# Attention with the values stationary in the array's column halves, outputs transposed, probabilities divided before use, and one more pipeline step

## The reference

```python
def swa_sink_attention(x, w_qkv, b_qkv, sinks, w_out):     # 32 query heads of 64, 4 key/value heads
    h = x @ w_qkv + b_qkv
    ...
    scores = jnp.einsum('bnikgd,bnjkd->bnkgij', q, kb).astype(jnp.float32) * ATTN_HEAD_DIM ** -0.5
    ...                                                      # blocks of 128 tokens, window 128
    scores = jnp.where(valid[None, :, None, None], scores + bias[None, None], -jnp.inf)
    m = jnp.maximum(jnp.max(scores, axis=-1, keepdims=True), sink)
    p = jnp.exp(scores - m)
    probs = p / (jnp.sum(p, axis=-1, keepdims=True) + jnp.exp(sink - m))
    o = jnp.einsum('bnkgij,bnjkd->bnikgd', probs.astype(vb.dtype), vb)
    return o.reshape(B, S, ATTN_Q_WIDTH) @ w_out
```

## Time and profile before

| | |
|---|---|
| Median of three runs | 2091.2 us |
| The profiled execution | 2091.75 us, its span 2090.0 us |
| PE busy | 2066.4 us, 99% of the span |
| DVE, ACT busy | 1416.5 us (68%), 887.2 us (42%) |
| Granted TensorE clock, mean | 0.997 of full |
| Attention stage (first S to the last turned output) | 1141.4 to 1290.2 us |

### The profile page before, as it was taken

How to read it: one execution, slowest core, us unless ns; L and a number is a source line. 1 busy time by engine, 2 the same in 40 slices (tenths; PEclk the granted TensorE clock), 3 DMA queues, 4 the chain that set the end, 5 groups by cost and what they waited for, 6 DMA issues and landing times.

```text
span 2090.0 us, 27045 instructions
## 1 busy us (share of the span) xinstructions
PE 2066.4 (99%) x10886; PEld 1761.2 (84%) x10886; DVE 1416.5 (68%) x1589; ACT 887.2 (42%) x813; POOL 5.8 (0%) x10
## 2 busy tenths in 40 slices
PE   8999999999999999999999999999999999999997
PEld 7888888888888888888878888888888888888886
DVE  5445366867767677676786665786776777766768
ACT  4443434543434344344434554454343434434342
POOL 0000000000000000000000000000000000000000
PEclk9999999999999999999999999999999999999999
DMA  8664464755555655555545434566555555555552
GB/s 310 211 193 151 140 242 146 249 193 197 183 197 182 196 185 192 189 187 195 184 165 187 134 108 168 175 213 216 195 183 198 182 197 184 193 188 188 193 184 98
DMA packets 193915, 390.30 MB, mean 187 GB/s; under 512 B 6377, under 2 KB 8643, under 8 KB 192835
## 3 DMA queue, kind: packets, MB, share of 16 engines
q1 hardware_dynamic: 193571, 389.24, 55.8%
q10 hardware_dynamic: 288, 0.26, 0.0%
HBM read 387.12 MB, written 2.10 MB: 186 GB/s over the span
## 4 chain that ended last, share of the span: by engine, by line
PE 97%; DVE 2%; ACT 1%; DMA 0%; issue 0%; DVEq 0%; ACTq 0%
PE ps L1137 17%; PE ps L1140 17%; PE ps L1138 17%; PE ps L1150 13%; PE ps L1152 13%; PE ps L1151 13%; PE ps L1126 1%; PE ps L1493 1%; PE ps L1200 0%; PE ps L1476 0%; PE ps L1162 0%; PE ps L1127 0%; PE ps L1337 0%; PE ps L1469 0%; PE ps L1467 0%; PE ps L1466 0%
## 5 line engine op out<-in xcount | busy, mean ns | idle before, releaser
L441 ACT ACTIVATE w_hi<-raw 128x2048 fp32r<-128x2048 f32 x355 | 679.8, 1917 | 956.7 <-DMA raw<-ffn_w_in 519.9
L699 DVE TENSOR_TENSOR w_lo<-raw,w_hi 128x2048 fp32r<-128x2048 f32 x355 | 808.2, 2287 | 249.2 <-ACT w_hi L441 248.6
L1138 PEld LDWEIGHTS ps<-T,w_lo 128*128 128x128 f32 x3136 | 589.2, 188 | 138.3
L1137 PE MATMUL ps<-T,w_hi 128*128 128x512 f32 x1568 | 621.0, 396 | 0.0
L1140 PE MATMUL ps<-T,w_hi 128*128 128x512 f32 x1568 | 620.2, 396 | 0.0
L1138 PE MATMUL ps<-T,w_lo 128*128 128x256 f32 x3136 | 616.1, 278 | 0.0
L1137 PEld LDWEIGHTS ps<-T,w_hi 128*128 128x128 f32 x1568 | 297.7, 190 | 4.5 <-issue 3.7
L1140 PEld LDWEIGHTS ps<-T,w_hi 128*128 128x128 f32 x1568 | 293.8, 187 | 0.0
L1150 PE MATMUL ps<-w_hi,gT 128*128 128x512 f32 x672 | 261.5, 389 | 0.0
L1152 PE MATMUL ps<-w_hi,gT 128*128 128x512 f32 x672 | 261.4, 389 | 0.0
L1151 PE MATMUL ps<-w_lo,gT 128*128 128x512 f32 x672 | 261.4, 389 | 0.0
(11 more groups left out here) (135 smaller groups left out, 971.1 us busy)
## 6 DMA issues: line engine op xcount, KB each, us to landing
raw<-ffn_w_in SPq DMA_DIRECT2D x176, 1024.0 KB, 5.0
raw<-ffn_w_out SPq DMA_DIRECT2D x88, 1024.0 KB, 5.0
raw<-even_w_in SPq DMA_DIRECT2D x39, 1024.0 KB, 5.1
raw<-attn_w_qkv SPq DMA_DIRECT2D x20, 1024.0 KB, 5.2
raw<-even_w_out SPq DMA_DIRECT2D x16, 1024.0 KB, 5.1
raw<-attn_w_out SPq DMA_DIRECT2D x16, 1024.0 KB, 5.0
arena<-ln_gain SPq DMA_DIRECT2D x4, 1024.0 KB, 7.0
arena<-ln_bias SPq DMA_DIRECT2D x4, 1024.0 KB, 9.0
```

The source lines that it names most:

```text
L441: nc.scalar.activation(w_hi[:, s % RING], raw[:, s % RING], ACT.Copy).then_inc(hi_ready, 1)
L699: vec.tensor_tensor(w_lo[:, s % RING], raw[:, s % RING], w_hi[:, s % RING].bitcast(F32), ALU.subtract).then_inc(lo_ready, 1)
L1137: mm(ps[:, bank], w_hi[:, s % RING, k, c], T[:, t], start=first, stop=False)
L1138: ins = mm(ps[:, bank, 0:SEQ], w_lo[:, s % RING, k, c], T[:, t, 0:SEQ], start=False, stop=False)
```

## The change

V swaps its operands: the values are stationary (64 columns, so half of the array's columns) and `PT` moves (128 columns). The two heads of a pair take the two column halves: their outputs go to partitions 0 to 63 and 64 to 127 of a bank, one bank for each block of queries. The result is thus already transposed, and one DVE copy takes it to `oT`; the 32 turns of the output on PE are gone. Since the sum's reciprocal now would belong to columns, DVE divides the exponentials by their sums before T (new semaphore `att_normed`), and V comes a burst later (pair b-3, T pair b-2), with `S` in two buffers. The output projection's first four tiles go to `gT`, its order and banks change, the splits of the output read `oT`, and the copy of the last query tiles' first half starts from a semaphore of its own.

```diff
-ODD_OUT_ORDER = [(0, 0), (0, 1), (1, 0), (1, 1), (0, 2), (1, 2), (2, 0), (0, 3), (1, 3), (2, 1), (2, 2), (2, 3)] + \
+ODD_OUT_ORDER = [(0, 0), (1, 0), (0, 1), (1, 1), (0, 2), (1, 2), (2, 0), (2, 1), (0, 3), (1, 3), (2, 2), (2, 3)] + \
...
-ODD_OUT_BANKS = [0, 2, 6, 0]
-ODD_OUT_ENDS = {8: 0, 9: 1, 12: 2}
+ODD_OUT_BANKS = [0, 2, 4, 0]
+ODD_OUT_ENDS = {9: 0, 10: 1, 12: 2}
...
-ATT_FILL_AT = {0: 0, 1: 2, 4: 4, 6: 6}
+ATT_FILL_AT = {-7: [0], -5: [1], 0: [2, 3], 1: [4], 3: [5], 5: [6], 7: [7]}
...
-BURSTS = PAIRS + 2
+BURSTS = PAIRS + 3
...
+        att_tiles = lambda j: (gT if j < 2 else T)[:, 2 * j:2 * j + 2]
...
-                act.wait_ge(used, ended + turn * 12)
+                if n == TP_ODD + 7:
+                    act.wait_ge(queries_half, 1)
+                else:
+                    act.wait_ge(used, ended + turn * 12)
...
-                if 0 <= b - 1 < PAIRS:
-                    act.wait_ge(att_turned, b)
+                if 0 <= b - 2 < PAIRS:
+                    act.wait_ge(att_turned, b - 1)
                     nc.scalar.activation(PT, ps[:, 6:8, 0:3 * P], ACT.Copy).then_inc(att_pt, 1)
+                for j in ATT_FILL_AT.get(s - S_ODD_OUT, ()):
+                    act.wait_ge(att_out, 2 * j + 2)
+                    if j >= 2:
+                        act.wait_ge(used, S_ODD_OUT)
+                    nc.scalar.activation(att_tiles(j)[:, :, 0:SEQ], oT[:, 2 * j:2 * j + 2], ACT.Copy).then_inc(t_hi, 1)
...
                 if 0 <= b - 1 < PAIRS:
-
-                    dve.wait_ge(att_exp, b)
-                    chain(vec.tensor_tensor(es[:, b - 1], rs[:, b - 1], es[:, b - 1], ALU.add))
-                    chain(vec.reciprocal(rinv[:, b - 1], es[:, b - 1]))
-                if 0 <= b - 2 < PAIRS:
-                    p = b - 2
+                    p = b - 1
+                    dve.wait_ge(att_exp, p + 1)
+                    chain(vec.tensor_tensor(es[:, p], rs[:, p], es[:, p], ALU.add))
+                    chain(vec.reciprocal(rinv[:, p], es[:, p]))
+                    for blk, (lo, n) in enumerate(((0, P), (P, 2 * P))):
+                        at = S[:, p % 2, :, lo:lo + n]
+                        ins = vec.tensor_tensor(at, at, rinv[:, p, :, blk].unsqueeze(2).to_broadcast([P, 2, n]),
+                                                ALU.mult)
+                    ins.then_inc(att_normed, 1)
+                if 0 <= b - 3 < PAIRS:
+                    p = b - 3
                     dve.wait_ge(att_mixed, p + 1)
...
-                    for a in range(2):
-                        o = AD * (2 * p + a)
-                        ins = vec.tensor_tensor(o_nat[:, :, o:o + AD],
-                                                ps[:, 6 + a, 3 * P:4 * P].rearrange("p (b n) -> p b n", b=2),
-                                                rinv[:, p, a].unsqueeze(2).to_broadcast([P, 2, AD]), ALU.mult)
-                    ins.then_inc(att_out, 1)
+                    vec.tensor_copy(oT[:, p].rearrange("p (b n) -> p b n", b=2), ps[:, 6:8, 3 * P:4 * P]) \
+                        .then_inc(att_out, 1)
+
+            def attention_low(s):
+
+                for j in ATT_FILL_AT.get(s - S_ODD_OUT, ()):
+                    dve.wait_ge(t_hi, FILL_ATT + j + 1)
+                    vec.tensor_tensor(att_tiles(j)[:, :, SEQ:2 * SEQ], oT[:, 2 * j:2 * j + 2],
+                                      att_tiles(j)[:, :, 0:SEQ].bitcast(F32), ALU.subtract).then_inc(t_ready, 1)
...
-                if 0 <= b - 2 < PAIRS:
-                    p = b - 2
+                if 0 <= b - 3 < PAIRS:
+                    p = b - 3
                     pe.wait_ge(att_pt, p + 1)
                     if p >= 1:
                         pe.wait_ge(att_out, p)
-                    for a in range(2):
-                        lo, kv = 3 * P, slice(AD * (p // 4), AD * (p // 4) + AD)
-                        mm(ps[:, 6 + a, lo:lo + AD], PT[:, a, 0:P], av[:, 0, kv], start=True, stop=True)
...
+                    kv, lo = slice(AD * (p // 4), AD * (p // 4) + AD), 3 * P
+                    for blk, key, i, start, stop in ((0, 0, 0, True, True), (1, 0, 1, True, False), (1, 1, 2, False, True)):
+                        for a in range(2):
+                            ins = mm(ps[AD * a:AD * a + AD, 6 + blk, lo:lo + P], av[:, key, kv],
+                                     PT[:, a, P * i:P * i + P], start=start, stop=stop)
                     ins.then_inc(att_mixed, 1)
-                if 0 <= b - 1 < PAIRS:
-                    pe.wait_ge(att_exp, b)
+                if 0 <= b - 2 < PAIRS:
+                    p = b - 2
+                    pe.wait_ge(att_normed, p + 1)
...
-            values_and_transposes(S_ODD_OUT - 1 - ATT_AT)
-            pe.wait_ge(added, TP_ODD + 9)
-            turn_output(0)
-            turn_output(1)
-            scores(S_ODD_OUT - 1 - ATT_AT)
...
-                if kg == 0 and n == 3:
+                if kg == 0 and n < 2:
+                    pe.wait_ge(added, TP_ODD + 8 + n)
+                elif kg == 0 and n == 2:
+                    pe.wait_ge(att_biased, PAIRS)
+                elif kg == 0:
                     pe.wait_ge(proj_added, NCH + 1)
...
-                projection(s, n, kg, ODD_OUT_BANKS[n], kg == 0, kg == KG - 1)
+                projection(s, n, kg, ODD_OUT_BANKS[n], kg == 0, kg == KG - 1, in_g=kg == 0)
...
-                    turn_output(2)
-                    turn_output(3)
```

More of the change, by code:

```diff
@@ L88, in fill_bank, with turns @@
 def fill_bank(n):
-    if FILL_ATT <= n < FILL_LN2:
-        return ATT_FILL_BANKS[n - FILL_ATT]
     return 4 + n % 4
+def turns(n):
+    return n - ATT_FILLS if n >= FILL_LN2 else n
 TP_EVEN = 0
@@ L199, in build_trunk @@
         akT = take(KVH, SEQ)
-        o_nat = take(TOK, D)
+        oT = take(KT, SEQ)
         av = take(TOK, KVH * AD)
-        S = take(2, 3 * P)
+        S = take(2, 2, 3 * P)
         PT = take(2, 3 * P)
@@ L271, in build_trunk @@
         att_exp = sem("att_exp")
+        att_normed = sem("att_normed")
+        queries_half = sem("queries_half")
         att_turned = sem("att_turned")
@@ L467, in norm_high @@
                 a, q = divmod(u, NCH)
-                act.wait_ge(turned, n + 1)
+                act.wait_ge(turned, turns(n) + 1)
                 nc.scalar.activation(T[:, GK * q:GK * q + GK, P * a:P * a + P],
@@ L644, in attention @@
                         for blk, (lo, n) in enumerate(((0, P), (P, 2 * P))):
-                            nc.scalar.activation(S[:, a, lo:lo + n], S[:, a, lo:lo + n], ACT.Exp,
+                            nc.scalar.activation(S[:, b % 2, a, lo:lo + n], S[:, b % 2, a, lo:lo + n], ACT.Exp,
                                                  bias=nm[:, b, a, blk:blk + 1],
@@ L664, in _ @@
                         halves(TP_ODD + 1 + 2 * cc + q, q_bank(cc) + 2 * q, s)
[L665 to L668, removed]
                 attention(s)
@@ L1041, in attention_max @@
                 dve.wait_ge(att_biased, b + 1)
-                vec.tensor_reduce(m_pair[:, b, :, 0], S[:, :, 0:P], AX_X, ALU.max)
-                chain(vec.tensor_reduce(m_pair[:, b, :, 1], S[:, :, P:3 * P], AX_X, ALU.max))
+                vec.tensor_reduce(m_pair[:, b, :, 0], S[:, b % 2, :, 0:P], AX_X, ALU.max)
+                chain(vec.tensor_reduce(m_pair[:, b, :, 1], S[:, b % 2, :, P:3 * P], AX_X, ALU.max))
                 chain(vec.scalar_tensor_tensor(nm[:, b], m_pair[:, b], -1.0, neg_sink[:, 2 * b:2 * b + 2],
@@ L1095, in _ @@
                         ins.then_inc(added, 1)
-                if s - S_ODD_OUT in ATT_FILL_AT and s != S_ODD_OUT + 6:
-                    for t in (0, 1):
-                        j = ATT_FILL_AT[s - S_ODD_OUT] + t
-                        fill_low(FILL_ATT + j, j)
                 i = s - S_ODD_OUT
@@ L1463, in values_and_transposes @@
                         pe.wait_ge(att_out, p)
[L1464 to L1470 removed]
+                    kv, lo = slice(AD * (p // 4), AD * (p // 4) + AD), 3 * P
[3 more added lines that the diff above has]
+                                     PT[:, a, P * i:P * i + P], start=start, stop=stop)
                     ins.then_inc(att_mixed, 1)
[L1472 to L1473 removed]
+                if 0 <= b - 2 < PAIRS:
+                    p = b - 2
+                    pe.wait_ge(att_normed, p + 1)
                     for a in range(2):
                         for i in range(3):
[L1476 removed]
+                            ins = nc.tensor.transpose(ps[:, 6 + a, P * i:P * i + P], S[:, p % 2, a, P * i:P * i + P],
                                                       ident[:])
@@ L1512, in _ @@
                     ins = turned_tile(s, kg, q_bank(c) + j, j)
+                    if s == S_ODD_OUT - 1 and j == 1:
+                        ins.then_inc(queries_half, 1)
                 ins.then_inc(used, 1)
```

37 lines of the change are left out of this document (7 added, 30 removed).

## The result

| | before | changed kernel |
|---|---|---|
| Median | 2091.27 us (2089.02 to 2091.47, 4 runs) | 2079.45 us (2076.90 to 2080.04, 4 runs) |
| Ratio | | 0.9943, 95% interval 0.9931 to 0.9954 |
| Span of the profiled execution | 2090.0 us | 2078.2 us |
| First S to the first turn of the next norm | 199.9 us | 188.0 us |
| From that turn to the end | 748.65 us | 748.68 us |

A forecast was written before the change was run, and what follows sets the result against it. PE was taken to bound the kernel, busy for 99% of the span. Savings of 3.5 + 3.05 + 3.7 less 0.3 make 9.95 us, leading from the median 2091.2 to 2081.3 us, range 2078 to 2088.

The forecast's parts named there:

- Turns: On PE, 32 transposes of the attention's output go, at 0.109 us each: 3.5 us saved.
- Waits that came with the turns: PE's waits and delays at the last query step, first output step and last V go: 3.05 us saved.
- The reserve for new waits: 0.3 us counted against the change for a late first output step and the like.
- margin of a tenth: At the first output step: query additions end near 1234.95, the new burst at 1235.04.
- V: V on PE falls from 1.28 to 1.05 us in each of 16 bursts, giving back 3.7 us.
- DVE and ACT hidden: DVE's added 1.1 us per step stays under PE: 5.9 of 8.3 us, 7.8 where query tiles are added.
- slack of 8 us: T's wait for the division: it ends near 1233.5, while the T that needs it stands after 1241.
- A: Rival on V: column halves do not run side by side, V costs 1.71 us, total 2091.9 us; chance 0.10.
- C: Rival on V: each change of column half drains the array, V 2.7 us, total 2107.8 us; chance 0.05.
- D: Rival: DVE late where query tiles are added, PE waits 1 to 3 us, total 2083 to 2085; chance 0.05.
- B: Rival on V: part of the weight loads is bare, V 1.39 us, total 2086.7 us; chance 0.12.

The follow-up runs named there:

- e6: Changed kernel with 32 transposes of 128x128 put back on PE, two more in each T: 2082.92 us, stretch 191.5 us.
- e10: Changed kernel with PE again waiting, between T and S of the last query step's burst, until all query tiles are added: stretch 189.5 us against 188.0.
- e9: Changed kernel without the early start of the last query tiles' first copy; ACT waits for the whole step: stretch 188.0 us, as in the changed kernel.
- e2: Changed kernel with both heads' V in the same column half, their results added up: 2090.09 us, stretch 10.4 us longer.
- e3: Changed kernel with V's stationary operand 128 columns wide, so in the array's full form, heads' results added up: 2085.28 us, stretch 6.0 us longer.
- e5: Changed kernel with V and T each cut in two and interleaved, two more changes of the array's form per burst: 2083.90 us, stretch 4.5 us longer.
- e7: Changed kernel with the pipeline one step shorter (T takes pair b-1, V pair b-2), the division still ahead of T: 2099.68 us.
- e4: Changed kernel with the burst in the order S, V, T in place of V, T, S, and one more DVE wait: 2079.52 us.
- e1: Changed kernel with V taking the first head's three matmuls, then the second head's, in place of alternating: 2081.39 us, stretch 4.2 us longer.
- e11: Changed kernel with V's matmuls in the order head 0, head 1 three times, head 0 twice: stretch 188.8 us against 188.0.
- e8: Changed kernel with burst order S, V, T, three buffers of `S`, and DVE's maxima ahead of its copy of V's result: 2076.76 us.

## Why the prediction was right

It forecast 2081.3 us, range 2078 to 2088; 2079.45 was measured. The mechanism is the one it named; of its 9.95 us two terms were too small, by 1.6 and 0.2, and one was not needed, 0.3. By its steps:

- **Turns**, 3.5 us: right. e6 put the same number of transposes back and paid 3.55.
- **Waits that came with the turns**, 3.05 us: the trace after shows none, and e10 got 1.5 of them back with one line. For that place the prediction had read 1.36 + 0.15. The other two are not tested singly; 11.94 - 3.55 - 5.3 leaves 3.1 for all waits, which is a remainder and no measurement. The prediction overlooked one small wait of the kernel before, behind the fourth output step, where S waits for DVE (L713) and T takes 0.94 us to it in place of 0.75:

```profile
1272.51 0.82 PE L1476 MATMUL ps<-ident,arena 128*128 128x128 f32 x6
1273.45 0.93 PE L1493 MATMUL ps<-arena 64*128 64x128 f32 x8
```

- **The reserve for new waits**, 0.3: not needed. The margin of a tenth at the first output step held. As the prediction read it, the new semaphore does not set the time of that copy (e9). The first output step asks for the first half alone, which DVE has added at 1230.54; the second is added at 1231.33, 0.7 us too late. That is read from the trace; no run makes this step wait for both.
- **V**, 1.05 us after: mis-sized by 0.10. It took 0.95, so 16 x 0.33 = 5.3 us came back and not 3.7. The mechanism was right on both counts: pairs side by side (e2 takes them away: +10.4), a price for the change of form (e3, e5). What was too high is the price within the new form. The second pass of a half starts late by 0.10 us in S (0.213 behind the first, the third 0.112 behind it) and by only 0.05 in V (0.160, then 0.109) and in T behind V (0.165, then 0.109). This goes with how long the weight loads last, 0.19 us in S and 0.14 in V and T, but no run varied that alone; it does not go with their columns, since T's have 128.
- **DVE and ACT hidden**: right, but closer than the sum had it. The prediction had 5.9 us of DVE in a step, 7.8 where it adds query tiles. The work added is as forecast, 1.2 against 1.1 us: over nine steps of the query projection DVE was busy for 5.5 us each, over eight of the changed kernel for 6.7 (two steps of either add tiles). But the sum began from 4.81, a light step, and behind the changeover DVE was busy for 7.96 us of 8.13 (rows below). The slack of 8 us that I gave T is one step wide: e7 takes that step away and loses 20 us, more than the change won. I had written it as a margin and not as a condition; it is one. The kernel before:

```profile
1155.22:1232.38 77.16, 77.16 (x523) 66.31 (x522) 49.91 (x105) 42.70 (x104) 0.00 (x0) 1.00 0.38 124
```

and the changed kernel:

```profile
1162.15:1228.19 66.04, 66.04 (x466) 53.34 (x465) 53.67 (x106) 38.97 (x95) 0.00 (x0) 1.00 0.39 128
1236.34:1244.47 8.13, 8.13 (x51) 6.22 (x51) 7.96 (x15) 5.77 (x16) 0.00 (x0) 1.00 0.36 129
```

- **Rivals.** A is e2, and came to within 2 us of its price (2090.1 against 2091.9): V costs 1.60 there, 1.45 and 0.15 around it, where A had 1.71. C had V cost 2.7 us with all around it; that is 0.95. D (DVE late) did not occur in the change, but did in e4, with 1.0 and 0.9 us of idle, as soon as PE's steps shrank by another 0.2. B would have shown V at about 1.15 us (six pairs of 0.165 and 0.16 for the form); it is 0.81, and its twelve weight loads fit beside the matmuls:

```profile
1162.15 0.64 PEld L1478 LDWEIGHTS ps<-arena 128*64 128x64 f32 x12 [0.25 <-issue]
```

The total of the parts, 3.5 + 3.05 + 5.3 = 11.85, or 12.0 with the wait that was overlooked, meets the measured 11.94.

## What to carry to other kernels

Where a product has 64 outputs and its weight loads set its pace, put the operand that is shared into column halves and let two products run beside each other; count the passes that overlap, 0.109 us for two in place of 0.22, and 0.3 us for going into the form and out (both measured here, with fp32 passes of 128 columns). Order small blocks of different form so that neighbours share a form, but look at who waits for the block that moves back: here 2.6 us of order were worth nothing until DVE's work was reordered too. And compare variants by a stretch between two marks of the trace where the whole time varies by more than the effect.

## What the runs showed that I had not expected

- Column halves are independent in order. With the heads one after the other (e1) the second half's first pass starts 0.27 us behind the first half's first, while three of the first half's six passes are still to start; with a nested order (e11) V is 0.87 us. So alternating the halves is worth 4.2 us here, but is no condition. Why the second half starts 0.27 us late in e1 and at once in e11 is not shown.
- Going from row halves to column halves directly costs no more than one change: with one change less in 13 bursts the stretch shrank by 2.6 us (e8), 0.2 for each.
- Three waits of 3.7 us on PE cost 6.5 us over their own length by the lower granted clock behind them (e7, 0.50 from 1166.6 to 1173.4). The same two waits of 1.85 and 1.41 us ahead of the attention brought the clock down in seven traces of thirteen and left it at 1.00 in six, so one trace does not tell what a wait costs.
